# First-layer residual: the output bias is folded into the rows by GpSimd, and VectorE's residual has two operations

## The reference, cut to what matters

```python
y = m @ w_out + b_out                        # merge_branches, m: gated sum of three branches
x  = layer_norm(alpha * x  + g_a  * y_lat, ln1_g, ln1_b)   # latent rows
xc = layer_norm(alpha * xc + gc_a * y_ctx, ln1_g, ln1_b)   # context rows, first layer only
h  = modulate(x, sh_f, sc_f)                 # layer_norm(x) * (1 + scale) + shift
```

## Time and profile before

| what | value |
|---|---|
| runs | 2640.31, 2640.54, 2640.99 us |
| profiled execution | 2643.34 us, its span 2641.5 us |
| TensorE busy | 2463.1 us, 93% of the span |
| mean granted clock | 0.972 of full |
| VectorE, ScalarE, GpSimd busy | 950.3, 664.4, 349.6 us |
| HBM traffic | 238 GB/s over the span, some 425 GB/s in the experts' stretches |

### The profile page before, as it was taken

The page is one execution under the profiler, slowest core; times in us unless marked ns, Lnnn a source line. Parts: engine busy times, 40 slices in busy tenths (PEclk is TensorE's granted clock), DMA queues, the critical chain, the costliest instruction groups (busy, mean ns, idle before and its releaser), DMA issues. The chain is left out here.

```text
span 2641.5 us, 32555 instructions
## 1 busy us (share of the span) xinstructions
PE 2463.1 (93%) x12921; PEld 1561.8 (59%) x12921; DVE 950.3 (36%) x1831; ACT 664.4 (25%) x1245; POOL 349.6 (13%) x403
## 2 busy tenths in 40 slices
PE   7999999999999898999998999999999898999996
PEld 4768666788888633443333758667888733443332
DVE  3335566622225730000003534566334741111113
ACT  3231445622222210110112521456333200000000
POOL 1241000000112220010001531000011220010001
PEclk9999999999999889999998999999999989999998
DMA  8671301323214599999998561004433799999995
GB/s 284 209 266 48 102 1 45 79 60 73 62 56 167 212 385 422 426 423 425 427 428 338 175 235 49 7 1 100 113 95 107 288 378 423 427 421 424 427 426 210
DMA packets 225084, 610.57 MB, mean 231 GB/s; under 512 B 63244, under 2 KB 145580, under 8 KB 190880
## 3 DMA queue, kind: packets, MB, share of 16 engines
q1 hardware_dynamic: 197250, 533.10, 52.9%
q0 software_dynamic: 24224, 62.75, 6.8%
q10 hardware_dynamic: 3456, 12.58, 1.3%
HBM read 585.96 MB, written 43.41 MB: 238 GB/s over the span
## 5 line engine op out<-in xcount | busy, mean ns | idle before, releaser
L1262 PE MATMUL slot<-arena 128*64 128x512 f32 (+2 forms) x3232 | 815.0, 615 | 62.5 <-DMA arena<-in_w_up_e 42.9
L1262 PEld LDWEIGHTS slot<-arena 128*64 128x64 f32 (+2 forms) x3232 | 295.7, 146 | 528.8 <-issue 520.1
L791 PE MATMUL abank<-round,round 128*128 128x512 f32 (+1 forms) x1792 | 491.9, 355 | 9.8 <-DVE round L1535 4.7
L791 PEld LDWEIGHTS abank<-round,round 128*128 128x128 f32 x1792 | 318.0, 189 | 73.2 <-issue 15.4
L791 PE MATMUL abank<-hT_low,round 128*128 128x512 f32 (+1 forms) x896 | 317.6, 354 | 0.0
L791 PE MATMUL vbank<-round,round 128*128 128x512 f32 (+3 forms) x1248 | 288.9, 360 | 6.4 <-issue 5.2
L2150 DVE TENSOR_TENSOR arena<-slot,arena 128x512 f32<-128x512 f32 x76 | 52.5, 691 | 645.1 <-ACT arena L2560 372.6
L791 PEld LDWEIGHTS vbank<-round,round 128*128 128x128 f32 x1248 | 214.7, 189 | 40.9 <-issue 8.4
L791 PEld LDWEIGHTS abank<-hT_low,round 128*128 128x128 f32 x896 | 168.6, 188 | 23.8 <-issue 0.5
L1843 DVE TENSOR_TENSOR arena<-vbank,arena 128x512 f32<-128x512 f32 x72 | 43.4, 602 | 291.9 <-PE vbank L791 283.0
L2739 POOL TENSOR_TENSOR arena<-arena 128x512 f32<-128x512 f32 (+1 forms) x48 | 56.0, 1166 | 578.5 <-DVE arena L1843 578.5
(11 more groups left out here) (353 smaller groups left out, 2922.3 us busy)
## 6 DMA issues: line engine op xcount, KB each, us to landing
arena<-in_w_down_e SPq DMA_DIRECT2D x40, 2048.0 KB, 24.1
arena<-in_w_gate_e SPq DMA_DIRECT2D x40, 2048.0 KB, 27.1
arena<-in_w_up_e SPq DMA_DIRECT2D x40, 2048.0 KB, 25.5
arena<-in_w_up_e SPq DMA_DIRECT2D x48, 1024.0 KB, 17.5
arena<-in_w_down_e SPq DMA_DIRECT2D x48, 1024.0 KB, 30.2
arena<-in_w_gate_e SPq DMA_DIRECT2D x44, 1024.0 KB, 17.0
arena<-in_w_ada POOLq DMA_DIRECT2D x80, 512.0 KB, 4.9
arena<-in_w_in SPq DMA_DIRECT2D x48, 512.0 KB, 4.3
```

The lines of the kernel that those rows point to most:

```text
L791: last = pe.matmul(to, x, y, start=(k == 0 and q == 0), stop=(k == len(terms) - 1 and q == 2))
L1262: last = pe.matmul(to[at, cols], x[:, at], w[:, at_w, :], start=first, stop=final)
```

## The change

In the first layer only:

1. GpSimd waits for `b_out` and the gate rows. It makes `gb_ctx = b_out * ga1 / alpha` and, in place of `b_out`, `b_out * ga0 / alpha`: four operations of 128 x 1024.
2. GpSimd adds such a row to each of the six tiles of `x_sb` (`row_prepared`). Tiles 0 and 1 are done before its first deviation, tile n+2 after the second deviation of tile n. It counts them on `pool_sum`.
3. VectorE's `residual` is PSUM times gate row, a wait for the prepared tile, and `alpha * x + T`: two operations instead of three.
4. `gates_summed(L)` takes the place of `PS(L + 1)` where ScalarE and SyncE wait, with the same value there; `PS` counts the six additions more for the second layer.

```diff
+        gb_ctx = ar(144, D)
...
-            return sum(16 * len(qblocks(k)) for k in range(L))
+            return sum(16 * len(qblocks(k)) + (NTILES if k == 0 else 0) for k in range(L))
+
+        def gates_summed(L):
+
+            return PS(L) + 16 * len(qblocks(L))
...
-                    dve.tensor_tensor(T, s[:, :], rows["bout"], ALU.add).then_inc(slot_taken_v, 1)
-                    dve.wait_ge(slot_taken_v, before(L) + n + 1)
-                    link(dve.tensor_tensor(T, T, rows[f"ga{c}"], ALU.mult))
-                    if t < CTX_TILES:
-                        dve.wait_ge(x_in[0], 32)
+                    if L == 0:
+                        dve.tensor_tensor(T, s[:, :], rows[f"ga{c}"], ALU.mult).then_inc(slot_taken_v, 1)
+                        dve.wait_ge(slot_taken_v, before(L) + n + 1)
+                        dve.wait_ge(pool_sum, gates_summed(L) + n + 1)
                     else:
-                        dve.wait_ge(x_in[t - 1], 64 if L == 0 else 96)
+                        dve.tensor_tensor(T, s[:, :], rows["bout"], ALU.add).then_inc(slot_taken_v, 1)
+                        dve.wait_ge(slot_taken_v, before(L) + n + 1)
+                        link(dve.tensor_tensor(T, T, rows[f"ga{c}"], ALU.mult))
+                        dve.wait_ge(x_in[t - 1], 96)
...
+                def row_prepared(t):
+
+                    pool.wait_ge(x_in[t - 1] if t else x_in[0], 32 if t < CTX_TILES else 64)
+                    gb = gb_ctx if t < CTX_TILES else rows["bout"]
+                    pool.tensor_tensor(x_sb[:, t, :], x_sb[:, t, :], gb, ALU.add).then_inc(pool_sum, 1)
+                    st["sum"] += 1
+
+                if L == 0:
+                    pool.wait_ge(rows7_in, 48)
+                    for to, ga in ((gb_ctx, "ga1"), (rows["bout"], "ga0")):
+                        link(pool.tensor_tensor(to, rows["bout"], rows[ga], ALU.mult))
+                        link(pool.tensor_scalar(to, to, 1.0 / ALPHA, None, ALU.mult))
+                    for t in range(2):
+                        row_prepared(t)
                 for n, t in enumerate(qt):
                     by_act = t != qt[-1]
                     deviation(mv[:, t, 1:2], rstd[:, t:t + 1], by_act and sums_to(L, "s8", 2 * n + 1))
                     deviation(mv2[:, t, 1:2], rstd2[:, t:t + 1], by_act and sums_to(L, "s8", 2 * n + 2))
+                    if L == 0 and t + 2 < NTILES:
+                        row_prepared(t + 2)
```

More of the change, by code:

```diff
@@ L2456, in mt_early_up @@
                 def mt_early_up():
-                    act.wait_ge(pool_sum, PS(L + 1) - 2 * len(qb))
+                    act.wait_ge(pool_sum, gates_summed(L) - 2 * len(qb))
                     for n in range(2):
@@ L2514, in _ @@
                 wo_up(wo_last[0:1])
-                act.wait_ge(pool_sum, PS(L + 1))
+                act.wait_ge(pool_sum, gates_summed(L))
                 for n in range(2):
@@ L3051, in _ @@
                 load_wout(2, wout_last[:, 4:7, :], 4 * P, 512)
-                sp.wait_ge(pool_sum, PS(L + 1) - 1)
+                sp.wait_ge(pool_sum, gates_summed(L) - 1)
                 load_wout(2, wout_last[:, 7:8, :], 7 * P, 512)
-                sp.wait_ge(pool_sum, PS(L + 1))
+                sp.wait_ge(pool_sum, gates_summed(L))
                 def mod_row(dst, v, part):
```

## The result

The changed kernel takes 2653.29 us in the median of 13 runs (2644.0 to 2656.41), the kernel before 2640.99 in 13 runs of the same chip (2634.91 to 2648.0). The ratio is 1.0046, with an interval of 1.0036 to 1.0057: 12.1 us slower, where 2.4 was predicted; that is outside the range and beyond the dearest rival, which had +6.9. The profiled execution took 2653.29 us, its span 2651.5, which is 10.0 more than before.

What follows compares the result with a forecast made beforehand. The path was taken as VectorE over three tiles, TensorE's fifth projection, VectorE to the routing, then the experts. +2.9 and +2.0, less 1.25 twice, gave +2.4: 2643 us from 2640.54, forecast range 2641.5 to 2645, overall 2636.5 to 2648.

Steps and rivals of the forecast that it cites:

- the dearest rival: GpSimd's deviations come late in tiles 1 and 2, with the scaling at its upper bound: +6.9, 2647.4 us; late deviations 22%.
- the wait for tile 0: Start of the stage: VectorE's second operation waits for GpSimd's prepared tile 0 until 836.9.
- a hold of 1.98 us: GpSimd's wide addition holds VectorE's next operation at the shared port, 1.98 us each for tiles 1, 2 and 3.
- The wait for ScalarE's cast: Tiles 1 and 2: VectorE's L1815 must await ScalarE's cast, done at 844.40, some 0.2 us later.
- The cover of the last additions: Tile 5's addition falls into VectorE's 8.32 us idleness before 882.30, cost 0; that idleness also covers tile 4's hold.
- The scaling: GpSimd's scaling by a constant in the preparation: 1.4 us taken, between bounds of 0.90 and 2.36.
- TensorE's gap: TensorE starts tile 2's projection 3.5 us late, at 841.4; the later stall of 5.6 us hides this delay.
- Tile 0 and tiles 1 and 2: VectorE's first three tiles: +2.9 for tile 0, +1.0 for each of the next two, +4.9 at the router copies.
- the late-deviation rival: Addition to tile n+2 delays tile n+1's first deviation: 1.3 us in each of tiles 1 and 2, 2645.5 us; 22%.
- the give-back in tiles 4 and 5: VectorE, still behind TensorE there, saves 1.25 us in each tile, so the routing is +2.4 us late.
- The additions hold nobody up: Faster rival: GpSimd's additions do not hold VectorE and the clock stays up; -8.7, 2632 us; 15%.
- The stream counts: Slower rival: the ring's 3.2 us idle are gone, so the expert weights' start sets the end; +4.9, 2645.4 us; 8%.

Runs made afterwards that it cites:

- a1: Changed kernel, but VectorE makes the two products of gate row and bias before the first residual and GpSimd only adds the rows; ratio 1.0025, +6.6 us against before.
- a2: Changed kernel without the additions to tiles 2 to 5, so the bias is missing in those rows; ratio 1.0031, +8.2 us against before.
- b1: Kernel before with the bias row set to zero by VectorE in its idle time; ratio 1.0007, +1.8 us against before.
- c1: Kernel before without the three filler matmuls ahead of the first layer's last two routers; ratio 1.0007, +1.8 us against before.
- d1: Kernel before with four filler matmuls in TensorE's stall before the first router matmuls; ratio 0.9992, -2.1 us against before.
- the second execution: Changed kernel, nothing altered, profiled a second time; that execution took 2654.65 us.
- a4: Changed kernel with VectorE making the products, GpSimd additions only for tiles 0, 1, 4 and 5, three VectorE operations for tiles 2 and 3; ratio 1.0005, +1.3 us.
- f1: Kernel before, with GpSimd multiplying tiles 2 to 5 by one where the changed kernel has its additions; ratio 1.0032, +8.4 us against before.
- a3: Changed kernel with VectorE's two operations and none of GpSimd's added work, so the first layer lacks the bias; ratio 0.9993, -1.8 us against before.
- f2: Kernel before plus GpSimd's four preparing operations, results unused, and a multiplication by one on tiles 0 and 1, which VectorE awaits; ratio 1.0040, +10.6 us.
- f5: Four tiles prepared, no fillers before the last two routers, three in the first router's stall, plus two ahead of the fourth tile's transposes; ratio 1.0000, 0.0 us against before.

## Why the prediction was wrong, by its steps

*Right.* The direction and the three places: the wait for tile 0, a hold of 1.98 us (measured 2.03) in each of the next tiles, and TensorE late at the router copies. The wait for ScalarE's cast is there too (0.15, 0.2 predicted). The new first operation stays at 1.23 us; a1 and a2 show that the gap and the holds are two costs with two causes. The cover of the last additions holds: tile 5's, at 883.19, falls into VectorE's idleness.

*The scaling, mis-sized.* "I take 1.4" between 0.90 and 2.36; it takes 2.79, above the upper bound, which the prediction named as a sign of being wrong. Two of them, less the earlier start, make tile 0 ready at 839.0 instead of 836.9. The upper bound was no bound: the scaling with its one input is not shorter here than the two-input operation (2.39).

*TensorE's gap, mis-sized.* 3.5 us predicted, 5.11 measured, for the reason above. The cover was right in kind: behind the gap the clock falls, which costs 1.6 us (23.49 - 21.9), and TensorE still waits 5.06 us for the copies afterwards, so it is VectorE's lateness that counts there.

*Tile 0 and tiles 1 and 2, mis-sized.* +2.9 predicted for the first tile, +4.55 measured. (Its 9.26 us before is a long one: b1, c1 and d1, equal up to there, have 8.40, 8.39 and 8.16, so the cost is 4.5 to 5.6.) +1.0 for each of the next two, +1.4 measured. The difference in the latter is the wait for the deviation, 0.51 us. That is the late-deviation rival: its condition is met, since the addition ends at 854.29 and L1926 (L1919 in the prediction) has begun at 852.06, but its price is 0.5 and not 1.3. Together: +4.9 predicted at the router copies, 4.55 + 2 x 1.42 = +7.4 measured from the first residual, and 7.98 with this execution's start, 0.6 later.

*The step that failed* is the give-back in tiles 4 and 5: "The routing is late by 4.9 - 1.25 - 1.25 = +2.4 us." VectorE did give back what that step says: the sixth tile's first operation comes 15.10 us after the fifth's, 16.74 before, and the last modulated rows are 4.6 late where the router copies were 8.0 late. But those rows do not set the routing. TensorE's own tail does, behind a projection that is 7.45 late: it turns the last rows 5.35 us after they are there, and it now runs in part at half clock, where the second of its four router products takes 3.63 us and the fillers 3.76. From the fifth tile's first operation, 7.45 late, to the gather the prediction had 2.5 us less than before's 44.05; it took 48.55, 4.5 more. Hence the 12.0 at the gather (8.5 in the second execution, with 46.49) and 10.0 to 12.1 at the end. The prediction took the clock of that stretch as given; it changed from 0.89 and 0.78 to 0.51 and 0.66. a4 shows the same from the other side: last rows 5.9 us early, clock 0.51, gather where it was.

The runs tell the two errors in this step apart. Four executions have the low clock in the sixth projection (12.76 to 12.78 us instead of 11.16) and full clock in the tail: f1 and b1 with three operations, a2 and a3 with two. The same stretch takes them 43.36, 43.01, 42.16 and 42.18 us. So with the clock laid the same way the two removed operations give back about 1.0 us and not 2.5. The rest is the clock, and that it falls there is not a matter of lateness alone. f1's projection ends as late as the changed kernel's, and the same instructions as at 909.86 and 913.29 above take:

```profile
909.37 1.98 PE L1121 MATMUL vbank<-arena 128*128 128x36 f32 x16 [0.73 <-ACT arena L2510]
911.18 1.96 PE L730 MATMUL slot<-cst 128*128 128x512 f32 x4
```

With the sizes put right and the old step kept, the sum would be 7.4 - 1.25 - 1.25 = +4.9, and with the start's 0.6, 5.5: less than half of the result. The step is worth more than the sizes.

*The rivals.* "The additions hold nobody up" is refuted by the holds, and it was priced too high: it let VectorE save 2.5 us in tiles 1 and 2, and a3 shows TensorE's pace taking part of that (its 860.7 for the end of that projection should also be 839.4 + 21.9 = 861.3). "The stream counts" does not hold in the profiled execution: the weights are 7.45 late but the first product 10.9, and it waits for VectorE. DMA is idle for longer than before in the stretch where the ring runs dry (share 0.80 over 945 to 975, 0.88 over 940 to 970 before).

*What stays open.* What decides where the clock's low stretch falls: both profiles of the changed kernel have it in the tail, and so have a1, a4 and f2, while f1, a2, a3 and b1 do not, and it moves the gather by over 2 us in one kernel. How much of the 12.1 us of the medians is the clock is therefore not shown; that the late preparation and the holds each make the kernel slower is. Open too is why a2 is 6.4 us slower than b1 with a gather 2.4 later, within intervals that leave some 4 us of room.

## What to carry to other kernels

Moving an elementwise operation from VectorE to GpSimd trades 1.25 us for a hold of 2.0 wherever VectorE reads two inputs from SBUF at that time, so the addition must be placed in VectorE's idleness, and the preparation must be finished before the first consumer: here two VectorE operations in an idle stretch did in 2.5 us what GpSimd did in 10.4. An operation taken off one engine is worth its time only where that engine is the last to be ready: here the routing waited for TensorE's tail of transposes and small matmuls, and two operations less on VectorE gave 1.0 us instead of 2.5. Such a tail has to be priced at both levels of the clock: a delay of 7.5 us ahead of it became 12.0 in one execution of the changed kernel, and in f1 one of 7.3 became 5.0. And a mark in one profiled execution is a hint: here it moves by 2 to 4 us on its own, and it should be set beside that execution's own time and not beside a median of others.

## What the runs showed of the hardware

- GpSimd's multiplication by a constant, one input of 128x1024, took 2.79 us, and the two-input multiplication of the same width 2.39. The Trainium skill (GPSIMD Engine Reference, Elementwise — side-by-side cycle accounting) has 1.03 cycles an element for bodies of up to two operations, by which the estimate is 0.9 us. The measurement decides.
- VectorE's operation with one input in PSUM is not held: at 833.22 it took 1.23 us while GpSimd's at 831.26 ran until 833.65 and the next began at 833.74. Every operation that was held (3.27, 3.31, 3.42, 3.00) reads two inputs in SBUF. The Trainium skill (SBUF — State Buffer, Who interferes with whom) says the same, and these rows agree.
- The hold works in both directions: in f2 GpSimd's scaling at 833.15 took 3.64 us beside VectorE's two-input operation at 832.89, and 2.79 at 827.79 with VectorE idle.
- Keeping TensorE busy at one place (d1) kept the clock at 1.00 there, and it was low behind the last projection instead (0.63 over 897 to 911). With fillers moved there too (f5) it was 1.00 over 892 to 905, and the last router matmuls, at 906.91, took the 3.63 us of 1.2 GHz. Without any filler moved, f1's tail had 1.00 where the changed kernel's, as late, had 0.51.
